# The products with the values move ahead of the second group of turns, in every step with more than four key blocks

## The chip, the cores and the metric

One Trainium2 chip; the program runs on one of its cores. The metric is the device time of one execution in microseconds (us), median over several. TensorE (PE in the rows) multiplies and transposes; its weight loads are shown apart (PEld). VectorE (DVE) and ScalarE (ACT) empty its accumulator banks (PSUM) and do the elementwise work, GpSimd (POOL) and SyncE (SP) play hardly any part here.

## What is computed

A trunk of two layers over 1024 frames of width 1024. Each layer is a mixer (attention), a norm, a mixture of 32 experts and a second norm. The change touches the attention alone:

```python
# layer 0, mixer B, 8 heads: stick breaking, strictly causal
z = einsum('bhqd,bhsd->bhqs', qb, kh) * scale
log_keep = where(causal, log_sigmoid(-z), 0.0)
later = cumsum(log_keep, axis=3, reverse=True) - log_keep
w = where(causal, exp(log_sigmoid(z) + later), 0.0)
y = einsum('bhqs,bhsd->bhqd', w, vh)
# layer 0, mixer A, 8 heads: window of 128 frames, softmax with sinks
# layer 1, mixer C, 16 heads: own chunk of 64 and the 8 before it
p = softmax(einsum('bqhd,bshd->bhqs', qc, kc) * scale + bias)
y = einsum('bhqs,bshd->bqhd', p, vc)
```

## The kernel before

**Pairs and steps.** Two heads make a pair (h = 0, 1). Each layer has eight pairs; layer 0 has four of kind "a" (pairs 0 to 3) and four of kind "b" (4 to 7), layer 1 has eight of kind "c". A pair goes through eight tiles of 128 queries, t = 0 to 7, and one tile of one pair is a step s, so a layer has 64 steps. A tile works on `blocks[t]` blocks of 128 keys: at most 2 for "a", t + 1 for "b", min(t, 4) + 1 for "c". More than four blocks (`high(pair, t)`) there are for t = 4 to 7 of the "b" pairs (5, 6, 7, 8 blocks) and of the "c" pairs (5 blocks).

**One step on TensorE** (the loop at L728). In this order: `scores(s + 1)` (L683, products of queries and keys of the next step, two heads on two halves of the array's rows); the pieces of projection of this step, `pieces[s][0]` (L664); `turn(s, h, "low")` (L695), which transposes the first four blocks of probabilities of each head into that head's bank; at t = 0 the transposes of the values (L704); `pieces[s][1]`; `turn(s, h, "high")`, which transposes blocks five and up into the same banks; and `apply(s - 1)` (L717), the products of the turned probabilities of the step before with the values, two heads on two halves of the array's columns.

**Projection pieces.** The next pair's K, Q and V are projected meanwhile. A job is one of them, has two halves g of 512 frames, and each half is 24 products in two parts of 12. All halves of the running loop go into one bank, `B_PROJ`; the first product of a half waits until the half before has been emptied (`proj_kept`, L657). With `FULL` (pairs 4 to 6 of layer 0, pairs 0 to 6 of layer 1) there is one piece in each of t = 0 to 3, before the low turns, and two in each of t = 4 to 7, one before and one behind them. Hence K's halves end in t = 1 and 3, Q's in t = 4 and 5, V's in t = 6 and 7. The last pair of each layer has no piece.

**The waits that matter.** A high turn waits for the copy of the low turn of its head out of the bank (`t_copied`), which ScalarE makes (L758). The copy of the high turn is made by ScalarE in "b" pairs and by VectorE in "c" pairs, in each engine's own fixed order of work. On ScalarE a step is: sigmoid (L817) or exponential (L806) of step s + 1; copies of the low turns; copies of the high turns for "b"; then `keep_half` of the half that ended in `pieces[s][1]`. On VectorE: the smallest score or the scan of step s + 1 (L904, L933); the scaling (L921); copies of the high turns for "c"; then `keep_half`; then `keep_y` (L942, L947) in every fourth step. `keep_half` empties a finished half: of Q and K ScalarE writes the high part (L787, L789) and VectorE then the low part (L867, L367); V is VectorE's alone (L878 for "c", L889 to L892 for "b"). The order on VectorE, as written:

```python
                    if high(pair, t) and pair.soft:
                        for h in range(2):
                            keep_turned(dve, dve.tensor_copy, s, h, "high")
                    for i, g in plan.halves_ended(s, 1):
                        keep_half(i, g)
```

Of the kernel before, what the change touches and what calls it, by code (L numbers as in the profile page):

```python
# [201 lines left out]
def build(nc, x, ab_w_in, ab_w_out, ab_sinks, t5_bias, c_w_in, c_w_out, c_rel_bias, ln_gain, ln_bias,  # L202
          moe_w_group, moe_b_group, moe_w_router, moe_b_router, moe_w_gate, moe_w_up, moe_w_down, out):
    ctx = ExitStack()
    with ctx:
        def sb(name, shape, dt=F32):
            return ctx.enter_context(nc.sbuf_tensor(name, shape, dt))
# [20 lines left out]
        def bank(b, n=1):  # L228
            return psum[:, b * BANK:(b + n) * BANK]
# [7 lines left out]
        plan = sb("plan", [P, EXTRA + 2], I32)  # L237
# [278 lines left out]
        def attention(layer, lead):  # L516
# [3 lines left out]
            plan = LAYERS[layer]  # L520
# [10 lines left out]
            def w_slot(i):  # L531
                return i if i < plan.first else i % 2
# [51 lines left out]
            def need(eng, sem, n):  # L584

                if n > 0:
                    eng.wait_ge(sem, n)
# [23 lines left out]
            def high(pair, t):  # L611
                return pair.blocks[t] > 4

            def job_bank(i, g):
                return bank(6 + plan.nth[i, g] % 2 if i < plan.first else B_PROJ)

            def half_cols(g):
                return slice(g * BANK, (g + 1) * BANK)
# [30 lines left out]
            def _(pe):  # L649
                def project(i, g, part):  # L650

                    steps = ((w_hi[w_slot(i)], x_hi), (w_hi[w_slot(i)], x_lo), (w_lo[w_slot(i)], x_hi))
                    for a in range(12 * part, 12 * part + 12):
                        k, c = a // CH, a % CH
                        if a == 0:
                            n = plan.nth[i, g]
                            need(pe, proj_kept, n - (1 if n <= 2 * plan.first else 0))  # L657
                            need(pe, hi_ready, i + 1 - lead.early)
                            if i == 0 and g == 0:
                                lead.half_ready(pe)  # L660
                        if k == 2 and c == 0:
                            need(pe, lo_ready, i + 1 - lead.early)
                        w, xs = steps[k]
                        mm = pe.matmul(job_bank(i, g), w[:, c * P:(c + 1) * P], xs[:, c, half_cols(g)],  # L664
                                       start=(a == 0), stop=(a == 23))
                    if part == 1:
                        mm.then_inc(proj_done, 1)

                def scores(s):
                    pair, t = plan.at(s)  # L670
                    if t == 0:
                        pe.wait_ge(proj_kept, plan.needed(pair.n))
                    for h in range(2):
                        need(pe, s_read[h], s)
                    b, kv, k0 = pair.n % 2, pair.kv, pair.key0(t)
                    places = [score_pieces(pair, t, h) for h in range(2)]
                    done = [None, None]
                    for a, w in places[0][1]:
                        for k, (qs, ks) in enumerate(((q_hi, k_hi), (q_lo, k_hi), (q_hi, k_lo))):
                            for h in range(2):  # L680
                                own = slice(DH * h, DH * (h + 1))
                                at = places[h][0] + a
                                done[h] = pe.matmul(psum[:, at:at + w], qs[b][own, t * P:(t + 1) * P],  # L683
                                                    ks[kv][own, k0 + a:k0 + a + w], start=(k == 0), stop=(k == 2))
                    for h in range(2):
                        done[h].then_inc(s_ready[h], 1)

                def turn(s, h, what):
                    pair, t = plan.at(s)
                    g = 0 if what == "low" else 1  # L690
                    if what == "low":
                        pe.wait_ge(p_ready[h], s + 1)
                    need(pe, t_copied[h], plan.group[s][what])
                    for b in range(4 * g, min(pair.blocks[t], 4 * g + 4)):
                        mm = pe.transpose(bank(B_TURN + h)[:, (b - 4 * g) * P:(b - 4 * g + 1) * P],  # L695
                                          probs_of(s, h)[:, b * P:(b + 1) * P], ident[:])
                    mm.then_inc(t_ready[h], 1)

                def turn_values(s, h):
                    pair, _ = plan.at(s)  # L700
                    pe.wait_ge(proj_kept, 2 * plan.index[V, pair.n] + 2)
                    need(pe, t_copied[h], plan.group[s]["values"])
                    for j in range(4):
                        mm = pe.transpose(bank(B_TURN + h)[:, j * P:(j + 1) * P],  # L704
                                          v_t[:, (4 * h + j) * P:(4 * h + j + 1) * P], ident[:])
                    mm.then_inc(t_ready[h], 1)

                def apply(s):
                    pair, t = plan.at(s)
                    if t % 4 == 0:  # L710
                        need(pe, y_kept, s // 4)
                    for h in range(2):
                        pe.wait_ge(t_copied[h], plan.groups_to(s))
                    kt = pair.key0(t) // P
                    for b in range(pair.blocks[t]):
                        for h in range(2):
                            mm = pe.matmul(bank(B_OUT)[DH * h:DH * (h + 1), (t % 4) * P:(t % 4 + 1) * P],  # L717
                                           v_r[pair.kv][:, (kt + b) * P + DH * h:(kt + b) * P + DH * (h + 1)],
                                           probs_t[s % 2][h][:, b * P:(b + 1) * P],
                                           start=(b == 0), stop=(b == pair.blocks[t] - 1))  # L720
                    mm.then_inc(o_ready, 1)
# [6 lines left out]
                for s in range(plan.steps):  # L728
                    pair, t = plan.at(s)
                    if s == 0:  # L730
                        for piece in plan.pieces[s][0]:
                            project(*piece)
                    if s + 1 < plan.steps:
                        scores(s + 1)
                    if s > 0:
                        for piece in plan.pieces[s][0]:
                            project(*piece)
                    for h in range(2):
                        turn(s, h, "low")
                    if "values" in plan.group[s]:  # L740
                        for h in range(2):
                            turn_values(s, h)
                    for piece in plan.pieces[s][1]:
                        project(*piece)
                    if high(pair, t):
                        for h in range(2):
                            turn(s, h, "high")
                    if s > 0:
                        apply(s - 1)
                apply(plan.steps - 1)  # L750

# [1843 lines left out]
```

## Time and profile before

| | |
|---|---|
| median of 3 runs | 2416.93 us (2415.77 to 2417.67) |
| the profiled execution | 2409.14 us, its span 2407.4 us |
| TensorE busy | 2309.6 us, 96% of the span |
| VectorE busy | 1793.6 us, 75% |
| ScalarE busy | 1364.6 us, 57% |
| mean granted TensorE clock | 0.990 of full |

TensorE's busy time counts a product from its start to the end of its pass through the array, so neighbours overlap; what one instruction costs TensorE in a dense stretch is the distance from its start to the next one's start. "Idle before" is time in which the engine had nothing under way.

### The profile page before, as it was taken

What the parts mean: (1) busy time and instruction counts of PE and PEld (TensorE: products, weight loads), DVE (VectorE), ACT (ScalarE), POOL (GpSimd) and SP (SyncE); (2) the same over time, 40 slices, a digit from 0 to 9 for tenths busy, and PEclk for the clock granted to TensorE, in tenths of its full rate; (3) what the DMA queues carried; (4) which work ended last, traced back from release to release, by engine and by line L of the source; (5) the groups of instructions that cost most, each with busy time, mean ns of one, the idle gap of its engine ahead of it and who ended that gap; (6) DMA issues with size and microseconds to landing.
All of it is one profiled execution on the core that took longest, in us unless ns stands there. A gap on an engine that the chain in (4) does not pass through costs nothing. (4 is left out here: it accounts for less than half of the span.)

```text
span 2407.4 us, 34223 instructions
## 1 busy us (share of the span) xinstructions
PE 2309.6 (96%) x12932; PEld 1885.3 (78%) x12932; DVE 1793.6 (75%) x2538; ACT 1364.6 (57%) x1690; POOL 271.4 (11%) x243
## 2 busy tenths in 40 slices
PE   8999998989999999998899999998989999999997
PEld 6777886878888888886677777776878888888884
DVE  4565556678999999998554555556679999999996
ACT  3454446126777777775344444444047777777763
POOL 0000000002212112111500000000011111111104
PEclk9999999999999999999999999999999999999999
DMA  4010003329999999999211111104159999999986
GB/s 132 24 32 27 27 10 106 126 109 362 389 384 379 387 384 385 389 387 340 102 40 45 38 38 38 38 36 169 45 191 405 395 398 399 388 378 380 373 339 265
DMA packets 156078, 534.40 MB, mean 222 GB/s; under 512 B 40160, under 2 KB 80120, under 8 KB 106760
## 3 DMA queue, kind: packets, MB, share of 16 engines
q1 hardware_dynamic: 136784, 498.46, 54.6%
q0 software_dynamic: 18496, 33.60, 3.7%
q8 instruction: 107, 1.75, 0.3%
q14 instruction: 59, 0.48, 0.1%
q10 hardware_dynamic: 632, 0.10, 0.0%
HBM read 515.23 MB, written 50.41 MB: 235 GB/s over the span
## 5 line engine op out<-in xcount | busy, mean ns | idle before, releaser
L367 DVE TENSOR_TENSOR arena<-arena,arena 128x2048 fp32r<-128x2048 f32 (+1 forms) x458 | 956.9, 2119 | 65.8 <-ACT arena L1991 51.1
L1991 ACT CAST arena<-arena 128x2048 fp32r<-128x2048 f32 x384 | 717.0, 1919 | 152.6 <-PE psum L1710 116.2
L1710 PE MATMUL psum<-arena,arena 128*128 128x512 f32 x3072 | 733.1, 394 | 0.1
L1710 PEld LDWEIGHTS psum<-arena,arena 128*128 128x128 f32 x3072 | 569.0, 189 | 114.3 <-issue 0.4
L664 PE MATMUL psum<-arena,arena 128*128 128x512 f32 x2016 | 503.4, 400 | 6.3 <-DVE arena L367 6.2
L664 PEld LDWEIGHTS psum<-arena,arena 128*128 128x128 f32 x2016 | 367.6, 188 | 99.5 <-issue 11.4
L1721 PE MATMUL psum<-arena,arena 128*128 128x512 f32 x1536 | 359.6, 390 | 2.8 <-DVE arena L367 2.8
L1721 PEld LDWEIGHTS psum<-arena,arena 128*128 128x128 f32 x1536 | 288.0, 188 | 64.0 <-DVE arena L367 4.0
L367 DVE TENSOR_TENSOR arena<-psum,arena 128x512 fp32r<-128x512 f32 (+1 forms) x186 | 160.2, 870 | 104.9 <-ACT arena L789 55.3
L806 ACT ACTIVATE arena<-arena,arena 128x640 f32<-128x640 f32 (+4 forms) x192 | 120.0, 626 | 203.7 <-DVE arena L904 152.9
L1207 PE MATMUL psum<-arena,arena 128*128 128x512 f32 x768 | 187.9, 401 | 8.7 <-ACT arena L363 6.9
L758 ACT COPY arena<-psum 128x512 f32<-128x512 f32 (+3 forms) x288 | 119.6, 467 | 113.8 <-PE psum L695 113.2
L358 PEld LDWEIGHTS psum<-ident,arena 128*128 128x128 f32 x1024 | 141.9, 194 | 44.4 <-issue 22.2
L1207 PEld LDWEIGHTS psum<-arena,arena 128*128 128x128 f32 x768 | 144.6, 192 | 39.6 <-issue 7.3
L1808 POOL DMA_INDIRECT arena<-x_rows,slot_rows x64 | 119.4, 1866 | 486.8 <-DMA expert_rows<-arena,slot_rows 449.0
L358 PE MATMUL psum<-ident,arena 128*128 128x128 f32 x1024 | 145.5, 281 | 29.4 <-DMA arena<-x_rows,slot_rows 15.1
L695 PE MATMUL psum<-ident,arena 128*128 128x128 f32 x888 | 130.9, 277 | 15.5 <-ACT arena L758 10.1
L695 PEld LDWEIGHTS psum<-ident,arena 128*128 128x128 f32 x888 | 105.7, 141 | 44.2 <-ACT arena L758 14.0
L904 DVE CUSTOM_DVE_ANT_0 arena<-psum,arena 128x640 f32<-128x640 f32 (+3 forms) x192 | 104.9, 572 | 29.1 <-PE psum L683 28.7
L717 PE MATMUL psum<-arena,arena 128*64 128x128 f32 x1776 | 125.7, 281 | 0.0
L1813 POOL DMA_INDIRECT expert_rows<-arena,slot_rows x64 | 64.2, 1003 | 477.9 <-DVE arena L2146 468.3
L683 PE MATMUL psum<-arena,arena 64*128 64x320 f32 (+5 forms) x1056 | 115.0, 338 | 2.5 <-DVE arena L904 1.3
(194 smaller groups left out, 1660.1 us busy)
## 6 DMA issues: line engine op xcount, KB each, us to landing
arena<-in_moe_w_gate SPq DMA_DIRECT2D x128, 1024.0 KB, 8.6
arena<-in_moe_w_up SPq DMA_DIRECT2D x128, 1024.0 KB, 7.8
arena<-in_moe_w_down SPq DMA_DIRECT2D x128, 1024.0 KB, 6.9
arena<-expert_rows SPq DMA_DIRECT2D x32, 512.0 KB, 11.1
x_rows<-arena SPq DMA_DIRECT2D x24, 512.0 KB, 2.6
arena<-in_c_w_in SPq DMA_DIRECT2D x24, 512.0 KB, 4.0
arena<-x_rows SPq DMA_DIRECT2D x24, 512.0 KB, 8.5
arena<-in_x SPq DMA_DIRECT2D x16, 512.0 KB, 6.9
```

Source lines behind the costliest of these rows:

```text
L358: m = pe.transpose(dst_bank[:, j * P:(j + 1) * P], rows[:, c0 + j:rows.shape[1]:stride], ident[:])
L367: return eng.tensor_tensor(tile, src, high.bitcast(F32), ALU.subtract)
L664: mm = pe.matmul(job_bank(i, g), w[:, c * P:(c + 1) * P], xs[:, c, half_cols(g)], start=(a == 0), stop=(a == 23))
L695: mm = pe.transpose(bank(B_TURN + h)[:, (b - 4 * g) * P:(b - 4 * g + 1) * P], probs_of(s, h)[:, b * P:(b + 1) * P], ident[:])
L717: mm = pe.matmul(bank(B_OUT)[DH * h:DH * (h + 1), (t % 4) * P:(t % 4 + 1) * P], v_r[pair.kv][:, (kt + b) * P + DH * h:(kt + b) * P + DH * ...
L758: copy(probs_t[s % 2][h][:, a:b], bank(B_TURN + h)[:, 0:b - a]).then_inc(t_copied[h], 1)
L806: act.activation(probs_a[s % 2][h][:, 0:ahead + nk], biased[h][:, 0:ahead + nk], ACT.Exp, bias=low[s % 2][h], scale=-1.0, accum_out=rowsum ...
L1207: return pe.matmul(bank(2 * (t % 2) + half), ys[:, c, t * P:(t + 1) * P], w[:, c, half * BANK:(half + 1) * BANK], start=(k == 0 and c == 0 ...
L1710: mm = pe.matmul(bank(o), cs[:, c * P:(c + 1) * P], ws[:, c * FF:(c + 1) * FF], start=(k == 0 and c == 0), stop=(k == 2 and c == CH - 1))
L1721: mm = pe.matmul(bank(B_Y + s), hs[:, c * P:(c + 1) * P], ws[:, c * D + s * BANK:c * D + (s + 1) * BANK], start=(k == 0 and c == 0), stop= ...
L1808: pool.indirect_dma_start(out=rows[b], out_offset=None, in_=x1_dram, in_offset=bass.IndirectOffsetOnAxis(ap=token, axis=0), bounds_check=S ...
L1991: act.copy(w_hi[w][:, cols], self.raw[w][:, cols]).then_inc(hi_ready[w], 1)
```

## The change

In each step with more than four blocks, except the last of a layer, `apply(s - 1)` is issued between `pieces[s][1]` and the high turns instead of behind them. It is one block of products moved past another on TensorE; no instruction is added or removed, and nothing changes on the other engines. It concerns 15 steps of layer 0 and 31 of layer 1.

```diff
@@ -742,10 +742,13 @@
                             turn_values(s, h)
                     for piece in plan.pieces[s][1]:
                         project(*piece)
+                    ahead_of_high = high(pair, t) and s + 1 < plan.steps
+                    if ahead_of_high:
+                        apply(s - 1)
                     if high(pair, t):
                         for h in range(2):
                             turn(s, h, "high")
-                    if s > 0:
+                    if s > 0 and not ahead_of_high:
                         apply(s - 1)
                 apply(plan.steps - 1)
```

## Rows read from the trace of the kernel before

**Rows 1.** Busy time by stretch: both attention stages, and one of low clock.
```profile
core 0: us, PE busy (x) PEld busy (x) DVE busy (x) ACT busy (x) POOL busy (x), PEclk, DMA share, GB/s
1200.00:1605.00 405.00, 401.45 (x2830) 322.38 (x2830) 207.02 (x589) 175.48 (x402) 3.50 (x24) 1.00 0.13 37
250.00:370.00 120.00, 119.04 (x882) 95.98 (x880) 62.08 (x74) 49.59 (x97) 0.00 (x0) 1.00 0.09 24
1622.80:1629.60 6.80, 6.28 (x38) 5.07 (x38) 3.85 (x9) 1.56 (x3) 0.00 (x0) 0.50 0.00 0
```
**Rows 2.** TensorE's waits, 1200 to 1605 us: total us, times, longest.
```profile
PE psum L704 <- ACT arena L758: 3.5, 7, 1.5
```
**Rows 3.** TensorE's waits, 1200 to 1646 us.
```profile
PE psum L695 <- ACT arena L758: 6.4, 6, 2.3
```
**Rows 4.** TensorE's waits, 240 to 404 us.
```profile
PE psum L695 <- ACT arena L758: 3.8, 4, 1.5
```
**Rows 5.** Timeline, layer 1, a step t = 6: start, length, engine and line.
```profile
1422.56 0.39 PE L664 MATMUL psum<-arena,arena 128*128 128x512 f32 x1
1422.79 0.38 PE L695 MATMUL psum<-ident,arena 128*128 128x128 f32 x2
...
1423.10 0.49 DVE L758 COPY arena<-psum 128x128 f32<-128x128 f32 x2 [2.66 <-PE psum L695]
...
1423.10 1.31 PE L717 MATMUL psum<-arena,arena 128*64 128x128 f32 x20
...
1423.50 0.68 DVE L878 COPY arena<-psum 128x512 f32<-128x512 f32 x1
...
1424.34 0.55 PE L683 MATMUL psum<-arena,arena 64*128 64x128 f32 x6
...
1424.82 0.50 PE L664 MATMUL psum<-arena,arena 128*128 128x512 f32 x1
```
**Rows 6.** Timeline of TensorE, layer 0, from a projection straight to scores.
```profile
51.58 0.39 PE L664 MATMUL psum<-arena,arena 128*128 128x512 f32 x1
51.90 0.33 PE L683 MATMUL psum<-arena,arena 64*128 64x128 f32 x2
```
**Rows 7.** Timeline, layer 0, pair 6, step t = 5.
```profile
344.58 0.60 PE L695 MATMUL psum<-ident,arena 128*128 128x128 f32 x4
...
344.99 0.65 ACT L758 COPY arena<-psum 128x256 f32<-128x256 f32 x2 [2.34 <-PE psum L695]
...
345.52 0.62 ACT L787 ACTIVATE arena<-psum 128x512 fp32r<-128x512 f32 x1
346.17 0.69 DVE L867 SCALAR_TENSOR_TENSOR arena<-psum,arena 128x512 fp32r<-128x512 f32 x1 [3.09 <-ACT arena L787]
...
346.35 1.65 PE L683 MATMUL psum<-arena,arena 64*128 64x512 f32 x12
...
347.93 0.50 PE L664 MATMUL psum<-arena,arena 128*128 128x512 f32 x1
```
**Rows 8.** Timeline, layer 0, pair 7: products of t = 4, scans of t = 7.
```profile
382.12 1.09 PE L717 MATMUL psum<-arena,arena 128*64 128x128 f32 x16
...
383.15 1.49 PE L683 MATMUL psum<-arena,arena 64*128 64x448 f32 x12
...
391.77 4.47 DVE L933 TENSOR_TENSOR_SCAN arena<-arena,arena 128x1024 f32<-128x1024 f32 x2 [2.21 <-ACT arena L817]
```
**Rows 9.** Timeline, layer 1, pair 7: TensorE in t = 4 to 7.
```profile
1624.21 1.98 PE L717 MATMUL psum<-arena,arena 128*64 128x128 f32 x16
...
1626.11 1.97 PE L683 MATMUL psum<-arena,arena 64*128 64x320 f32 x12
...
1633.22 1.15 PE L683 MATMUL psum<-arena,arena 64*128 64x320 f32 x12
...
1638.27 1.31 PE L717 MATMUL psum<-arena,arena 128*64 128x128 f32 x20
...
1639.51 1.09 PE L695 MATMUL psum<-ident,arena 128*128 128x128 f32 x8
```

## The prediction

> **What bounds the kernel now.** I read the page first (TensorE 96% busy), then busy time by stretch, TensorE's waits, and last the timeline of single steps. The steps that the change touches are of two sorts. In pairs that have projection pieces TensorE is never out of work: 401.45 of 405 us busy in layer 1, 119.04 of 120 in layer 0's "b" pairs [rows 1], and its only waits in layer 1 there are for the turn of the values at t = 0 [rows 2]; none stands ahead of a projection piece or a high turn. There the distance between the starts of TensorE's instructions is the time, and whatever adds to it is paid in full. In the last pair of each layer there is no piece between low and high turns, and the high turn waits for ScalarE's copy of the low one: 6.4 us in 6 waits in layer 1 [rows 3] and 3.8 in 4 in layer 0 [rows 4] (the last step of each layer, which the change leaves out, has part of these). So 40 changed steps (4 of each of 3 + 7 pairs) have no wait to fill, and 6 have one (t = 4, 5, 6 of the two last pairs).
>
> **A. One change of array form more, 40 steps.** Projection and turns use the array as one tile of 128 by 128, products with the values as 128 by 64, scores as 64 by 128. Before, a step goes projection, high turns, products, scores: two changes of form. After, it is projection, products, high turns, scores: three. What a change costs is in the distances. Projection to high turn, same form: 1422.56 to 1422.79, 0.23 us [rows 5]. Projection to products does not occur before; the nearest is projection to scores, 51.58 to 51.90, 0.32 [rows 6]. That is 0.09 more. Twenty products then take the same 1.24 up to the next start whether scores or turns follow (1423.10 to 1424.34 [rows 5], 1638.27 to 1639.51 [rows 9]), so the way back to turns costs as much as the way to scores did. But the first turn behind a change has no weights loaded yet: eight turns last 1.09 there [rows 9], against 0.38 for two in [rows 5], which makes 0.11 a turn and 1.04 for eight; 0.05 more. From high turns to scores I take the 0.20 between forms that I also have between turns and products (two turns 0.11 apart, then 1423.10 [rows 5]). Sum 0.14 a step, 40 x 0.14 = 5.6 us. Bounds: 0 if the new change is hidden like the 0.23, and 0.18 if both sides of the turns paid 0.09; I take 0.14 as each part has a row of its kind.
>
> The row shows 0.32 against 0.23. The Trainium skill (TensorEngine Tiling (Array Packing), Tiling Modes, Key Properties) says that going from one tiling mode to another drains TensorE; the trace agrees, by 0.09 us. The skill has the opposite rule too: TensorE: Matmul & The Clock Gate, Part 2, has the next weights loaded early, behind a running product, into the spare weight buffer; by it the added change would be free (rival 2).
>
> **B. V's halves in layer 1, 14 steps.** This is what becomes late. In a "c" pair VectorE copies the high turns first and then empties the projection bank, and the next piece waits for that. In the step of [rows 5] the last projection product starts at 1422.56. The products with the values now start at 1422.88 (+0.32) and the turns 1.24 later, 1424.12 and, 0.11 and the 0.05 of A behind it, 1424.28. VectorE's first copy started 0.31 after the first turn, and the copy of V ended 1.08 after that (1423.50 + 0.68 - 1423.10), all back to back: 1424.12 + 0.31 + 1.08 = 1425.51, and some 0.06 for the semaphore, 1425.57. TensorE gets there at 1424.28 + 0.20 + 0.48 for the six scores (1424.34 to 1424.82) = 1424.96. It waits 0.61. Before, the copy of V ended at 1424.18, 0.64 ahead of need: the cover was products and scores, and the scores alone are too short. The next piece starts 0.75 late in all, of it 0.14 from A. At t = 7 the six scores are over 256 columns, some 0.06 longer: wait 0.55 (estimate). 7 x (0.61 + 0.55) = 8.1 us. A wait can't be less than nothing and can't much exceed copies and V's copy laid behind the last turn without scores, 1.1: bounds 0 and 15.
>
> **C. Q's halves in layer 1, 14 steps.** Same order, but VectorE's part takes 0.69 [rows 7] and the scores behind are twelve, 1.08 (1.15 [rows 9] less the overlap of 0.07). Counted from the first high turn, the bank is free at 0.31 + 0.40 (both copies, less their overlap with what follows [rows 5]) + 0.69 + 0.06 = 1.46, and TensorE needs it at 0.16 + 0.20 + 1.08 = 1.44. Wait 0.02: 0.3 us.
>
> **D. Q's halves in layer 0, 6 steps.** Here ScalarE copies the high turns and then writes Q's high part, VectorE's low part follows. In [rows 7] the last projection product starts 0.23 ahead of the first turn, 344.35, so the products start at 344.67, the turns at 345.91, 346.07, 346.18, 346.29. The chain of copy, 0.62, 0.03, 0.69 ran from 344.99 to 346.86; the first copy started 0.30 after its second turn. Now it runs from 346.37 to 348.24, free at 348.30. TensorE is there at 346.29 + 0.20 + 1.58 (346.35 to 347.93) = 348.07. Wait 0.23; t = 4, with shorter copies and shorter scores, is taken as the same. 6 x 0.23 = 1.4 us. V in layer 0 has no wait: VectorE does not copy high turns there.
>
> **E. Layer 0's last pair.** Products fill the wait between low and high turns. They take 1.03 at t = 4 (382.12 to 383.15 [rows 8]) and 1.24 at t = 5; the waits ahead of the high turns are of that size and longer (up to 1.5 [rows 4]). Both are saved, 2.3 us. At t = 6 TensorE would save 1.4 more, but the low turn of t = 7 then waits for VectorE's scans, 4.47 us for two from 391.77 on [rows 8], which start only as much earlier as scores and sigmoid do, 2.3. So 2.3 us; bounds 1.0 and 3.7.
>
> **F. Layer 1's last pair.** The ring is scores, smallest score, exponential, copy of the low turn, high turn, products, next scores. VectorE had idle time in it, so taking the products out saves their length each time: 1.03 + 1.24 + 1.24, less 0.2 at t = 6 for the copies of the high turns, which the next low turn must await: 3.3 us. Besides, the granted clock fell to 0.50 from 1622.8 to 1629.6 [rows 1], 1.2 instead of 2.4 GHz, after TensorE had waited 2.3 us [rows 3]; sixteen products took 1.98 instead of 1.09 [rows 8, 9] and twelve scores 1.97 instead of 1.15 [rows 9]. That is 1.7 us which comes back if the clock stays up, and with the longest wait cut from 2.3 to 1.3 I think that it does, though runs may differ.
>
> **Sum.** A 5.6 + B 8.1 + C 0.3 + D 1.4 = 15.4 us lost; E 2.3 + F 3.3 = 5.6 won, 7.3 with the clock. Net +8.1 to +9.8; I take +9. This is made on the profiled execution (2409.14 us, 2407.4 of span; what lies around the span does not change) and added to the median, which stands 7.8 above it: 2416.9 + 9 = 2426 us.
>
> VectorE and ScalarE have other work behind the late copies: the smallest score and the exponential of step s + 2, later by up to 1 us. They are needed one projection piece (3 us) and more later, and stay hidden. `keep_y` is needed a step later too.
>
> **The rivals.**
> 1. The bank is emptied in time (no B, C, D). For it: VectorE is busy only 207 of 405 us [rows 1]. Against it: the order on VectorE is fixed, and the 0.48 of scores is shorter than copies plus V's copy. It decides at 0.84 us behind the first high turn at t = 6 (0.16 + 0.20 + 0.48): a bank that is free by then costs nothing, and my sum has it free at 1.45. Then 5.6 - 5.6 to 7.3, that is 0 to -1.7: 2415 to 2417, not slower. Chance 0.10.
> 2. The added change of form is free. Then the turns and their copies come 0.14 earlier as well, waits stay and A goes: 15.4 - 5.6 = 9.8 lost, 6.4 won, +3.4: 2420 us. For it only that the same-form distance is hidden. Chance 0.08.
> 3. The last pairs give nothing back, as another engine takes over the wait there (in layer 0 VectorE is near it): +15.4, 2432 us. For it: E is already cut short by the scans. Against: VectorE stood idle 2.21 us ahead of those scans [rows 8]. Chance 0.07.
> 4. Faster by more than 0.2%: the rings of E and F shorten by the full waits and no wait appears elsewhere, with A at its low bound: 7 to 9 us gained, 2409. Chance 0.04.
> The forecast has the rest, 0.71, with its own range 2422 to 2430 (B off by a third either way, the clock of F, the spread of 1.9 us between runs).
>
> **How the numbers follow.** 0.2% of the time, 4.8 us, is about what a measurement of this kernel can tell from no change. Faster: rival 4, 0.04, and a little of rival 1: 0.05. Same (2412.1 to 2421.7): the rest of rival 1, rival 2 and the low edge of the forecast: 0.17. Slower: 0.78. The range 2420 to 2431 takes in the forecast's own and rival 2.
>
> **What would show each step.** A: projection to products 0.32 and eight turns at 1.09 in every changed step; 0.23 or less would refute it. B: a new wait of TensorE, L664 for VectorE's L878, some 14 times, about 8 us. C and D: L664 for L867, up to 20 times, 2 us together, 0.23 each in layer 0. E and F: the waits of L695 for L758 in the last pairs down to about half, and each layer's last pair shorter by 2.3 and by 3.3 to 5.0 us; the clock at 1.00 through layer 1's last pair. The prediction is wrong if no new wait at L664 appears, or if the late smallest scores hold up a low turn (L695 for L921).

## The result and the profile after

The changed kernel takes 2422.89 us median (10 runs), the kernel before 2415.70 (10 runs); the ratio is 1.0038, 95% interval 1.0028 to 1.0048. That is 9.2 us slower by the ratio (6.8 to 11.6) and 7.2 by the medians. The forecast was +9 us and 2426 us. Of the 3 us between 2426 and the median 1.2 are the kernel before, which stands at 2415.70 here and not at the 2416.9 that the sum was added to, and the rest is 9 against 7.2. The profiled execution of the changed kernel took 2421.80 us, its span 2420.1, so 12.7 more than the profiled one before; two single executions also differ where nothing was changed (layer 0's first scores start 1.5 us later here, and 2.5 more come between the two attention stages), and so I compare stretches of the attention below. Lines behind L744 have moved by 3: L758 is now L761, L867 is L870, L878 is L881, L904 is L907.

TensorE's waits in the changed kernel, layer 1's attention, 1200 to 1660 us (total us, times, longest):

```profile
PE psum L664 <- DVE arena L881: 7.3, 13, 0.6
PE psum L704 <- ACT arena L761: 5.4, 8, 1.9
PE psum L695 <- ACT arena L761: 3.9, 8, 1.3
```

The first row is new: projection pieces wait for VectorE's copy of V, 13 times, 0.56 us each. The third answers to [rows 3]: over the whole stage the waits for the copy of a low turn are down from 6.4 to 3.9 us, the longest from 2.3 to 1.3; they are 8 now, because the 0.15 us of waiting for the second head's copy are listed in all four steps, where before they were listed at t = 6 and 7 only. The stretch of pairs 5 and 6 of layer 0, 260 to 372 us:

```profile
PE psum L664 <- DVE arena L870: 0.8, 4, 0.2
```

Q's low part, as D has it: four waits of 0.2 (0.23 at t = 4, 0.16 at t = 5); pair 4 has two more, 0.5 us together. Now the same step t = 6 as in [rows 5], in the timeline of the changed kernel (start, length, engine and line):

```profile
1432.24 0.39 PE L664 MATMUL psum<-arena,arena 128*128 128x512 f32 x1
1432.56 1.31 PE L717 MATMUL psum<-arena,arena 128*64 128x128 f32 x20
1433.81 0.44 PE L695 MATMUL psum<-ident,arena 128*128 128x128 f32 x2
1434.17 0.49 DVE L761 COPY arena<-psum 128x128 f32<-128x128 f32 x2 [3.33 <-PE psum L695]
1434.17 0.55 PE L683 MATMUL psum<-arena,arena 64*128 64x128 f32 x6
1434.58 0.68 DVE L881 COPY arena<-psum 128x512 f32<-128x512 f32 x1
...
1435.31 0.73 PE L664 MATMUL psum<-arena,arena 128*128 128x512 f32 x2 [0.59 <-DVE arena L881]
```

Read it from the top. Projection to products is 0.32 (before, projection to turns 0.23), products to turns 1.25, and two turns last 0.44 instead of 0.38, since the second starts 0.16 and not 0.11 after the first. VectorE's three copies are back to back as before, but the first starts 0.36 behind the first turn and not 0.31, and they now begin at the end of the step: V's copy ends at 1435.26, and TensorE, through with its six scores, starts the next piece at 1435.31. From the last projection product to the next piece it is 3.07 us; [rows 5] has 2.26, the forecast 3.01. A wait in brackets counts from the end of the last score's pass; the sum counted from where the next piece could have started, which is 0.48 behind the first score [rows 5], at 1434.65. So the piece is 0.66 late for a listed wait of 0.59. At t = 7 of the same pair the next piece starts thus:

```profile
1444.64 0.74 PE L664 MATMUL psum<-arena,arena 128*128 128x512 f32 x2 [0.52 <-DVE arena L881]
```

Its six scores start at 1443.50; before they took 0.54 up to the next piece (1432.87 to 1433.41), so this piece is 0.60 late.

The granted clock of the last pair, busy time by stretch of the changed kernel (columns as in [rows 1]):

```profile
1633.00:1652.00 19.00, 14.55 (x149) 11.29 (x150) 13.70 (x40) 10.80 (x25) 0.00 (x0) 1.00 0.01 1
1652.90:1656.40 3.50, 3.34 (x30) 3.11 (x31) 0.58 (x2) 0.12 (x1) 0.00 (x0) 0.54 0.03 5
```

The clock stays at 1.00 where it had fallen to 0.50 before, and falls a little later, at the last products of the pair. Their row, with the two last rows of the turns ahead of it:

```profile
1652.58 0.33 PE L695 MATMUL psum<-ident,arena 128*128 128x128 f32 x1 [0.24 <-ACT arena L761]
...
1653.07 0.43 PE L695 MATMUL psum<-ident,arena 128*128 128x128 f32 x1 [0.16 <-ACT arena L761]
1653.43 3.92 PE L717 MATMUL psum<-arena,arena 128*64 128x128 f32 x40
```

Forty products take 3.92; the same forty took 2.40 in the kernel before:

```profile
1641.59 2.40 PE L717 MATMUL psum<-arena,arena 128*64 128x128 f32 x40
```

### The profile page after: what moved, and what is told of

It is laid out like the page before. It is cut to its first block and busy times, and to the rows that moved or that the text cites. A ratio compares the mean times of both kernels' runs of the same rounds, so it can differ in the third digit from the quotient of the medians.

```text
span 2420.1 us, 34223 instructions
## 1 busy us (share of the span) xinstructions
PE 2319.1 (96%) x12932; PEld 1884.2 (78%) x12932; DVE 1789.5 (74%) x2538; ACT 1363.0 (56%) x1690; POOL 274.9 (11%) x243
## 5 line engine op out<-in xcount | busy, mean ns | idle before, releaser
L664 PE MATMUL psum<-arena,arena 128*128 128x512 f32 x2016 | 502.0, 399 | 14.6 <-DVE arena L881 7.3
L664 PEld LDWEIGHTS psum<-arena,arena 128*128 128x128 f32 x2016 | 366.8, 188 | 109.5 <-DVE arena L367 10.1
L761 ACT COPY arena<-psum 128x512 f32<-128x512 f32 (+3 forms) x288 | 119.6, 466 | 122.1 <-PE psum L695 121.6
L358 PE MATMUL psum<-ident,arena 128*128 128x128 f32 x1024 | 147.8, 285 | 29.2 <-DMA arena<-x_rows,slot_rows 17.1
L717 PEld LDWEIGHTS psum<-arena,arena 128*64 128x64 f32 x1776 | 95.9, 138 | 28.7 <-issue 27.7
L907 DVE CUSTOM_DVE_ANT_0 arena<-psum,arena 128x640 f32<-128x640 f32 (+3 forms) x192 | 104.7, 570 | 16.6 <-PE psum L683 16.2
```

The source lines that it names most:

```text
L358: m = pe.transpose(dst_bank[:, j * P:(j + 1) * P], rows[:, c0 + j:rows.shape[1]:stride], ident[:])
L761: copy(probs_t[s % 2][h][:, a:b], bank(B_TURN + h)[:, 0:b - a]).then_inc(t_copied[h], 1)
```

## The experiments

Each was timed beside the kernel before, e1 to e4 on one chip and e5 to e8 on another (the kernel before had 2415.24 and 2415.17 us there). The table has the ratio of each to it with the 95% interval, what that makes of 2415.2 us, and the number that was expected.

| kernel | median us | ratio (interval) | us by the ratio | expected |
|---|---|---|---|---|
| e1, last pairs only | 2408.04 | 0.9963 (0.9951 to 0.9974) | -8.9 | -5.6 |
| e2, whole change, bank emptied first | 2413.41 | 0.9989 (0.9977 to 1.0001) | -2.7 | 0 |
| e3, projecting pairs only | 2432.03 | 1.0063 (1.0046 to 1.0081) | +15.2 | +15.4 |
| e4, projecting pairs only, bank emptied first | 2420.16 | 1.0016 (1.0001 to 1.0032) | +3.9 | +5.6 |
| e5, bank emptied first, nothing else | 2414.99 | 1.0001 (0.9989 to 1.0013) | +0.2 | 0 |
| e6, e1 and the turn of the values | 2402.76 | 0.9947 (0.9929 to 0.9965) | -12.8 | -8 to -12 |
| e7, V's steps of layer 1 only | 2425.62 | 1.0050 (1.0031 to 1.0069) | +12.1 | +10 |
| e8, Q's steps of layer 1 only | 2416.31 | 1.0008 (0.9995 to 1.0020) | +1.9 | +2.5 |

The intervals are some 5 to 9 us wide. The parts can be told apart more finely in the profiled executions, between starts of scores on TensorE, which the lines of the timeline give. In us, worked out from those starts: "0: 4-6" is from the scores of step 33 to those of step 57 of layer 0 (pairs 4 to 6), "0: 7" from there to the scores of step 63; "1: 0-6" from the scores of step 1 to those of step 57 of layer 1, "1: 7" to step 63's, "1: end" from there to the start of the last product.

| kernel | 0: 4-6 | 0: 7 | 1: 0-6 | 1: 7 | 1: end |
|---|---|---|---|---|---|
| before | 181.69 | 22.80 | 398.31 | 28.42 | 10.50 |
| changed | 185.09 | 20.52 | 411.27 | 24.63 | 11.17 |
| e1 | 183.24* | 20.52 | 398.32 | 24.31 | 11.04 |
| e2 | 185.10* | 20.51 | 403.24* | 24.30 | 9.55 |
| e3 | 187.31* | 22.77 | 411.16 | 28.76 | 10.50 |
| e4 | 185.05* | 22.79 | 401.72 | 28.42 | 10.49 |
| e5 | 183.84* | 22.77 | 398.30 | 27.15 | 10.50 |
| e6 | 182.08* | 19.85 | 396.20 | 23.36 | 9.56 |
| e7 | 183.30* | 22.77 | 408.10 | 29.06 | 12.89 |
| e8 | 182.34* | 22.77 | 401.20 | 28.41 | 10.50 |

A star marks a stretch at whose start the granted clock was at 0.5 for a while in that execution, where it was not in the two profiles compared above.

**e1, the last pairs alone.**

```diff
-                    ahead_of_high = high(pair, t) and s + 1 < plan.steps
+                    ahead_of_high = high(pair, t) and s + 1 < plan.steps and not plan.pieces[s][1]
```

> The products move ahead of the high turns only where no projection piece stands between low and high turns: t = 4, 5, 6 of the last pair of each layer, 6 steps. My theory has all the loss in the other 40 steps and 2.3 + 3.3 us of gain here, so 5.6 us faster than before, perhaps 4 to 7, as the granted clock may rise or fall elsewhere in these pairs. TensorE's waits of L695 for ScalarE's copy fall from 6.4 to about 2.5 us in layer 1, none at L664 for VectorE's copy of V. Rival (the last pairs give nothing back, another engine takes over the wait): 0, within 1 us of before.

Faster by 8.9 us (6.3 to 11.8). Layer 1's other pairs are where they were (398.32), and the two last pairs have all of the gain that the changed kernel has there: 22.80 to 20.52 and 28.42 to 24.31. The rival that they give nothing back is refuted. In layer 1 TensorE's waits for the copies of the low turns fall from 6.4 to 3.9 us, not to the 2.5 that was expected (1200 to 1665 us):

```profile
PE psum L695 <- ACT arena L761: 3.9, 8, 1.3
```

In layer 0's last pair TensorE's waits are now these (240 to 404 us):

```profile
PE psum L704 <- ACT arena L761: 1.3, 3, 0.6
PE psum L695 <- DVE arena L936: 1.3, 1, 1.3
PE psum L695 <- ACT arena L761: 0.4, 2, 0.2
```

Of the 3.8 us for the copies [rows 4] 0.4 are left, and one wait of 1.3 for VectorE's scan has come, where E put it: 3.8 - 0.4 - 1.3 = 2.1 in listed waits, against 2.28 measured between the scores. That the scan takes back what is filled at t = 6 shows behind them: from the scores of step 63 to the last product of layer 0 it is 12.42 us before and 12.41 in e1. The stretches that the change touches account for some 6 us; what the rest of the 8.9 is, if it is more than the interval, they don't show.

**e2, the whole change, with the projection bank emptied ahead of the copies of the high turns** (the same on ScalarE):

```diff
+                    for i, g in plan.halves_ended(s, 1):
+                        keep_half(i, g)
                     if high(pair, t) and pair.soft:
                         for h in range(2):
                             keep_turned(dve, dve.tensor_copy, s, h, "high")
-                    for i, g in plan.halves_ended(s, 1):
-                        keep_half(i, g)
```

> The changed kernel, but VectorE and ScalarE empty the projection bank (keep_half) before they copy the high turns. My theory: the new waits at L664 (B, C, D, in the profile some 7.3 + 0.8 us and their share of longer starts, 9.8 us in the sum) go, the added change of array form (5.6 us) and the gain of the last pairs (5.6) stay, so about 0 against before, -2 to +1.5. Rival (the loss is not the bank but something else about the late turns, such as late smallest scores or late low turns): it stays 7 to 10 us slower than before.

TensorE's order is that of the changed kernel, and the loss is gone: 2.7 us below the kernel before (5.6 below to 0.2 above), so the rival of 7 to 10 us above it is refuted. All its waits from 1200 to 1620 us:

```profile
PE psum L704 <- ACT arena L761: 5.1, 8, 1.5
```

and its step t = 6, the one shown twice already:

```profile
1429.67 1.31 PE L717 MATMUL psum<-arena,arena 128*64 128x128 f32 x20
1429.78 0.69 DVE L881 COPY arena<-psum 128x512 f32<-128x512 f32 x1 [2.29 <-PE psum L664]
1430.92 0.44 PE L695 MATMUL psum<-ident,arena 128*128 128x128 f32 x2
1431.28 0.49 DVE L761 COPY arena<-psum 128x128 f32<-128x128 f32 x2 [0.81 <-PE psum L695]
1431.28 0.55 PE L683 MATMUL psum<-arena,arena 64*128 64x128 f32 x6
1431.77 3.00 PE L664 MATMUL psum<-arena,arena 128*128 128x512 f32 x12
```

V's copy now runs under the products and ends 1.3 us ahead of need; the piece follows the scores at once. The copies of the high turns are as late as in the changed kernel and hold up nothing.

**e3, the projecting pairs alone.**

```diff
-                    ahead_of_high = high(pair, t) and s + 1 < plan.steps
+                    ahead_of_high = high(pair, t) and s + 1 < plan.steps and bool(plan.pieces[s][1])
```

> The products move only in the 40 steps with a projection piece between low and high turns; the last pairs are as before. My theory: A + B + C + D = 15.4 us slower than before (14 to 17). Rival (the last pairs give nothing back): the same 7 to 9 us as the whole change.

Slower by 15.2 us (11 to 20), as A to D together. With e1 it adds up: 15.2 - 8.9 = 6.3 against 9.2 of the whole change, each of the three known to some 2 to 4 us only.

**e4, e3 with the bank emptied first** (both edits above).

> The products move in the 40 steps with a projection piece only, and the projection bank is emptied before the high turns are copied. What is left is the added change of array form alone, with no wait: 40 x 0.14 = 5.6 us slower than before (4.5 to 7). Rival (a change of form is hidden by early loading of weights): 0. Second rival (the bank is not the wait): 15 us, as without the new order on the other engines.

This leaves the added change of form. No wait at L664 is listed; all that is, 1200 to 1620 us:

```profile
PE psum L704 <- ACT arena L761: 5.1, 8, 1.5
```

It costs 3.9 us (0.2 to 7.7) by the ratio; layer 1's 28 steps take 3.41 us more, 0.12 each. The scores of successive steps show 0.14, 0.15, 0.12 and 0.11 more in the four steps of a pair, and 0.06 less in the one behind. Both rivals, 0 and 15 us, are out, the first by the stretches rather than by the ratio.

**e5, the control: only the order on VectorE and ScalarE.**

> The kernel before, with only the order on VectorE and ScalarE changed: keep_half ahead of the copies of the high turns; TensorE's order is untouched. A control for e2 and e4: my theory has no wait at the projection bank in the kernel before, so nothing to win, and the copies of the high turns are needed a projection piece later, so nothing to lose: within 1 us of before. Rival (emptying the bank first is a gain of its own, and e2 and e4 are quick because of it and not because a wait went): 5 us or more faster.

No difference (0.9989 to 1.0013), and 398.30 against 398.31 in layer 1. Emptying the bank first is worth nothing by itself; in e2 and e4 it was the wait that went. The 27.15 of its last pair, against 28.42, is the clock, which was at 0.50 only from 1630.6 to 1633.8 us there and not for 6.8 us.

**e6, e1 and the products ahead of the turn of the values.**

```diff
+                    ahead_of_values = "values" in plan.group[s] and s > 0
+                    if ahead_of_values:
+                        apply(s - 1)
                     if "values" in plan.group[s]:
                         for h in range(2):
                             turn_values(s, h)
...
-                    if s > 0 and not ahead_of_high:
+                    if s > 0 and not ahead_of_high and not ahead_of_values:
```

> e1, and besides apply(s - 1) stands ahead of the turn of the values at t = 0 of each pair that has one, where TensorE waits for ScalarE's copy of the low turn (0.3 us in most pairs, 0.6 and 1.5 in the two last). It adds a change of form (0.14 us) each time. Expected on top of e1: 0.2 us in each of 9 pairs and 0.5 and 1.3 in the two last, some 3 us; 8 to 12 us faster than before in all. Rival (the added forms eat the filled waits): the same as e1.

Faster than both kernels: 2402.76 us, 12.8 less than before (8.5 to 17.1). Over e1 it gains 2.1 us in layer 1's stretch of pairs 0 to 6, which has six turns of values that the edit reaches: 0.35 each. In the kernel before the first of these started 0.72 behind the first low turn (1436.31 and 1437.03 in pair 4), where two low turns take 0.22; 0.50 lost, less 0.14 for the added change of form, is 0.36, where 0.2 was expected. In the last pairs it is 0.67 and 0.95, expected 0.5 and 1.3. In layer 1's last pair the step itself is 1.24 shorter (3.50 us from the scores of step 57 to the next, 4.74 in e1), but the granted clock is at 0.50 from 1624.1 to 1627.3 us, inside the pair, and a later step is 0.28 longer for it. This is the same edit as the one studied, made where the trace has a wait.

**e7 and e8, V's and Q's steps of layer 1 alone.**

```diff
-                    ahead_of_high = high(pair, t) and s + 1 < plan.steps
+                    ahead_of_high = layer == 1 and t in (6, 7) and bool(plan.pieces[s][1])
```

(e8: `t in (4, 5)`.)

> The products move only at t = 6 and 7 of pairs 0 to 6 of layer 1, 14 steps, where V's halves end. My theory puts the greater part of the loss here: 8.1 us of waits at L664 for VectorE's copy of V and 14 x 0.14 = 2.0 for the form, 10 us slower than before (8 to 12). Rival (the loss is spread evenly over the 40 steps, 15.4 / 40 each): 5.4.

> The products move only at t = 4 and 5 of pairs 0 to 6 of layer 1, 14 steps, where Q's halves end and twelve scores hide the emptying of the bank. My theory: 2.0 us for the form and 0.3 to 1 of waits, 2.5 us slower than before (1.5 to 4). Rival (evenly spread): 5.4, as e7.

Fourteen steps each, and the cost is 12.1 (7.5 to 16.7) against 1.9 us (-1.2 to 4.8); in layer 1's stretch 9.79 against 2.89, which add up to 12.68 of the 12.96 of the whole change. An even spread is refuted. e7's waits, 1200 to 1620 us:

```profile
PE psum L664 <- DVE arena L881: 7.2, 13, 0.6
```

Nearly the 7.3 us of the whole change, from 14 of its 46 steps. e7's last pair (29.06 and 12.89) is long because the clock was at 0.50 three times in it, near 1640, 1649 and 1655 us; that is part of its 12.1 us. e8 has no listed wait of L664: its delay ends before the pass of the last score does, in which TensorE counts as busy (C below).

## Why the prediction was right, step by step

**The price of the form (A)** was 0.14 a step; measured 0.11 to 0.15 (e4), 0.12 on the whole, 3.4 us in layer 1 where the sum had 3.9. The distance itself is 0.32, as [rows 6] had it for another pair of forms. The Trainium skill's rule (TensorEngine Tiling (Array Packing), Tiling Modes, Key Properties) that a change of tiling mode drains TensorE agrees with that. The Trainium skill's rule of early weight loading (TensorE: Matmul & The Clock Gate, Part 2) holds inside a form, 0.23, and did not reach across; rival 2 is out. The rows of the weight loads show both. Before, the turns' weights were loaded from 1422.56 on, behind the last projection product that started then; in the changed kernel the load for the products with the values starts with the first of them, 0.32 behind the last projection product:

```profile
1422.56 0.37 PEld L695 LDWEIGHTS psum<-ident,arena 128*128 128x128 f32 x2
...
1432.56 1.07 PEld L717 LDWEIGHTS psum<-arena,arena 128*64 128x64 f32 x20 [0.35 <-issue]
```

**V's halves (B)** were to cost 0.61 and 0.55 of wait at t = 6 and 7; counted as the sum counts, the two steps shown have 0.66 and 0.60, which makes 7 x 0.66 + 6 x 0.60 = 8.2 us (estimate from the two) against 8.1; the 7.3 us of the list are the same waits without the pass of the last score. The agreement is in part luck. Each wait is some 0.05 longer than the sum had it, since the first copy starts 0.36 and not 0.31 behind a turn that follows a change of form, and there are 13 and not 14: no piece follows the last V. That last late copy costs 0.34 in another place. It stands ahead of VectorE's smallest score in the first step of pair 7, so the exponential, ScalarE's copies and the turn of the values (the wait of 1.9 at L704, 1.5 before) are late, and from the scores of step 57 to the next it is 5.08 us instead of 4.74. The prediction had said that the smallest scores stay hidden; here, where no piece covers them, they did not. e2 takes the wait away without touching TensorE, and the loss goes with it, so that this is the cause is shown, and so is rival 1's failure: the bank was not free in time.

**Q's halves (C)** cost some 0.07 of wait a step and not 0.02, 1 us instead of 0.3: from e8, 2.89 us less 14 x 0.14, over 14. The timeline has it directly: twelve scores took 1.07 up to the next piece before (1415.23 to 1416.30) and take 1.13 in such a step now (1424.87 to 1426.00). The missing 0.05 is that of the first copy again. **D** was 0.23 a wait. By the starts, t = 5 of pairs 5 and 6 is 0.23 late and the four others 0.30, 1.7 us in all against 1.4; pairs 4 to 6 of layer 0 took 3.40 us longer, the sum had 12 x 0.14 + 1.4 = 3.1.

**The last pairs.** E: 2.28 us measured, 2.3 forecast, with the scan as what cuts it short. F, the last pair of layer 1, was right in its mechanism and wrong in one term. Between the scores the gain is 28.42 - 24.63 = 3.79, which is 1.03 + 1.24 of products and 1.86 of the clock, less the 0.34 of the late copy of V; e1, which has no such copy, has 4.11. The next low turn, from the scores of step 63, is 0.92 us closer (1645.91 to 1651.28 now, 1633.22 to 1639.51 before, [rows 9], where F had 1.04). Then the clock falls anyway, and forty products cost 1.5 us more. So what the clock gave back is lost again but for 0.3: F is 3.1 in this execution, not 5.0. e1 falls on the forty products too (11.04), e2 behind the last product (9.55), and e6 once inside the pair and once behind the last product (9.56). Where the clock falls differs between kernels whose last pair runs in the same order, and no run here shows what decides it; the step that failed is the one that said a shorter longest wait keeps the clock up.

**The sum.** In the stretches: +3.40, -2.28, +12.96, -3.79, +0.67, together +11.0, where the forecast had +9.8 with no gain from the clock and +8.1 with it. The 1.2 between them: layer 1's stretch has 12.96 where A, B and C came to 12.3, layer 0's 3.40 where A and D came to 3.1, and the rest is F. The ratio over all executions says 9.2, the medians 7.2.

## What to carry to other kernels

A block of work that is moved into a dense stretch fills nothing; what it can do is delay what it is moved past. Follow the moved-past work to its reader in another engine's fixed order and ask what is queued behind it: here two small copies stood ahead of the emptying of a bank, and 1.25 us of products in front of them cost 0.6 us a step and more. Make the move only where the trace has a wait ahead of what the block is moved past, longer than what the added change of array form costs (0.14 us here); a wait of 0.50 was enough in e6. And compare delays by starts: a delay shorter than the pass of the last instruction is in no list of waits.

## What the runs showed of the hardware

In the traces before and changed the distance across a change of form is the same for each pair of forms seen: 0.32 us from a projection product to scores and to products with the values alike, and 0.20 from turns or products to any other form, where a turn follows a turn by 0.11. The low clock of layer 1's last pair was not removed by filling a 2.3 us wait to 1.3 but came later: it began 18 us behind the first scores of the stretch "1: 7" before, and 32 us behind them in the changed kernel, among the shorter waits at the pair's end; in e2 it fell behind the last product and cost nothing there, and in e6 it came 19 us behind the first scores, inside the pair, at a cost of 0.28 us. The low level is 1.2 GHz, the full one 2.4.
